# Order of choices, products and loads in the expert stage of a hybrid encoder layer

## The reference

```python
def _peer(hn, w_query, sub_keys, expert_u, expert_v):
    q = (hn @ w_query).reshape(B, S, PEER_HEADS, 2, PEER_HALF)
    s = jnp.einsum('bshpd,hpkd->bshpk', q, sub_keys)
    v1, i1 = lax.top_k(s[..., 0, :], PEER_TOPK)
    v2, i2 = lax.top_k(s[..., 1, :], PEER_TOPK)
    ...
    expert = e1 * N_KEYS + e2
    gate = jax.nn.softmax(cv, axis=-1)
    ...
        pre = jnp.einsum('tkd,td->tk', expert_u[it], xt)
        act = jax.nn.gelu(pre, approximate=False) * gt
        return jnp.einsum('tk,tkd->td', act, expert_v[it])
```

## Time and profile before

| | |
|---|---|
| three timed runs | 4036.6, 4049.0, 4050.2 µs; median 4049.0 |
| the profiled execution | 4044.4 µs, span 4042.7 µs |
| TensorE / its weight loads / VectorE / GpSimd / ScalarE busy | 92% / 79% / 66% / 48% / 31% |
| mean granted clock of TensorE | 0.964 |
| moved by DMA | 788.6 MB, mean 195 GB/s |

### The profile page before, as it was taken

The page is one execution under the profiler, slowest core; times in us unless marked ns, Lnnn a source line. Parts: engine busy times, 40 slices in busy tenths (PEclk is TensorE's granted clock), DMA queues, the critical chain, the costliest instruction groups (busy, mean ns, idle before and its releaser), DMA issues.

```text
span 4042.7 us, 55073 instructions
## 1 busy us (share of the span) xinstructions
PE 3721.7 (92%) x19212; PEld 3179.7 (79%) x19212; DVE 2684.3 (66%) x5197; ACT 1252.3 (31%) x1835; POOL 1939.3 (48%) x1352
## 2 busy tenths in 40 slices
PE   8978789999879899999999999999889999899998
PEld 6844478888767578799989999999667888677887
DVE  5443277776212437847878888788797666589996
ACT  3013233432211321233333333333233333333333
POOL 1023122222100013887878888888888888322220
PEclk9989889999989899999999999999889999999999
DMA  3259300000231024458888888888879999899996
GB/s 116 101 202 400 130 19 9 18 18 0 83 104 31 21 94 96 80 132 258 254 251 258 264 268 261 262 266 243 219 210 270 283 274 265 293 343 388 396 391 231
DMA packets 376333, 788.58 MB, mean 195 GB/s; under 512 B 137104, under 2 KB 245648, under 8 KB 342288
## 3 DMA queue, kind: packets, MB, share of 16 engines
q1 hardware_dynamic: 210320, 451.28, 32.8%
q0 software_dynamic: 165888, 336.01, 28.1%
HBM read 643.09 MB, written 144.05 MB: 195 GB/s over the span
## 4 chain that ended last, share of the span: by engine, by line
PE 28%; POOL 17%; issue 6%; DVE 5%; DMA 4%; DVEq 2%; ACT 1%; SPq 0%; POOLq 0%; ACTq 0%
PE peer_ps L2148 18%; POOL gates_d L2038 14%; PE peer_ps L2057 4%; PE peer_ps L2071 4%; POOL rows L2026 2%; POOL peer_rows L2026 2%; DMA peer_gat<-gates_d 2%; DMA rows<-in_expert_uv,peer_idx 1%; DMA late_in<-gates_d 1%; DVEq L2359 1%; PE peer_ps L2094 1%; DVE peer_acc L2444 1%; DVE late_rows L2429 1%; DVE late_in L2451 0%; DVEq L2443 0%
## 5 line engine op out<-in xcount | busy, mean ns | idle before, releaser
L2038 POOL DMA_INDIRECT gates_d<-peer_gates,peer_idx x768 | 1362.5, 1774 | 342.4 <-issue 222.8
L2057 PE MATMUL peer_ps<-high,peer_uh 128*128 128x384 f32 x2048 | 531.7, 340 | 58.3 <-DVE peer_ul L2346 51.7
L2057 PE MATMUL peer_ps<-low,peer_uh 128*128 128x384 f32 x2048 | 526.3, 338 | 0.0
L2057 PE MATMUL peer_ps<-high,peer_ul 128*128 128x384 f32 x2048 | 525.1, 337 | 0.0
L2057 PEld LDWEIGHTS peer_ps<-high,peer_uh 128*128 128x128 f32 x2048 | 371.3, 190 | 74.7 <-issue 67.5
L2057 PEld LDWEIGHTS peer_ps<-low,peer_uh 128*128 128x128 f32 x2048 | 375.3, 190 | 0.0
L2057 PEld LDWEIGHTS peer_ps<-high,peer_ul 128*128 128x128 f32 x2048 | 374.9, 190 | 0.0
L2148 PE MATMUL peer_ps<-peer_vh,peer_ah 128*128 128x512 f32 x1026 | 327.2, 401 | 46.0 <-DVE peer_al L2463 45.9
L2026 POOL DMA_INDIRECT late_rows<-in_expert_uv,peer_idx x108 | 135.9, 1258 | 407.4 <-DVE peer_acc L2444 365.0
L2148 PE MATMUL peer_ps<-peer_vh,peer_al 128*128 128x512 f32 x1026 | 323.2, 397 | 0.0
L2148 PE MATMUL peer_ps<-peer_vl,peer_ah 128*128 128x512 f32 x1026 | 321.7, 395 | 0.0
(11 more groups left out here) (470 smaller groups left out, 7694.9 us busy)
## 6 DMA issues: line engine op xcount, KB each, us to landing
late_in<-in_expert_uv SPq DMA_DIRECT2D x170, 512.0 KB, 4.9
gates_d<-mla_zeros POOLq DMA_DIRECT2D x128, 512.0 KB, 30.1
hidden_d<-peer_hid SPq DMA_DIRECT2D x128, 384.0 KB, 3.0
peer_raw<-in_expert_u SPq DMA_DIRECT2D x86, 512.0 KB, 4.9
peer_val<-in_expert_uv SPq DMA_DIRECT2D x86, 512.0 KB
late_in<-hidden_d SPq DMA_DIRECT2D x170, 192.0 KB, 5.3
late_in<-gates_d SPq DMA_DIRECT2D x170, 192.0 KB, 6.3
first_raw<-in_expert_u SPq DMA_DIRECT2D x42, 512.0 KB
```

Source lines behind the costliest of these rows:

```text
L2038: pool.indirect_dma_start(gates_flat, bass.IndirectOffsetOnAxis(ap=idx[:, n, k:k + 1], axis=0), gates[:, n, k:k + 1], None, compute_op=ALU ...
L2057: last = nc.tensor.matmul(ps[i][:, a, 0:HD], w[:, cols], x[:, kc, a * HD:(a + 1) * HD], start=(kc == 0 and w is uh[i % 2] and x is high), ...
```

## The change

- `unit_order`: within each head, the dense tiles come before the looked-up ones.
- `block_in` and `block_out`: all products of high by high parts (in `block_in` also low tokens by high weights) come first and wait for the high parts alone; the rest waits for the low parts.
- `load_out`: v and hidden values of block 129 (the second of pass 1) are loaded ahead of the gates of block 128.
- `halves(0)` and `others(0)`, the copies of pass 0's sums, stand one block sooner (before block 129's high parts instead of block 130's).
- Look-up 176, the first behind the last scatter, waits until block 129 is multiplied with its gates. The groups of rows from there on begin at slot 5 of pass 1 instead of 3 and come every 2.9 slots instead of 3.

```diff
@@ unit_order
-    return ([(head, tile) for head in range(PH) for tile in (looked_up if head < 5 else ()) + PASSES[0]]
-            + [(head, tile) for head in range(PH) for tile in (looked_up if head >= 5 else ()) + PASSES[1]])
+    return ([(head, tile) for head in range(PH) for tile in PASSES[0] + (looked_up if head < 5 else ())]
+            + [(head, tile) for head in range(PH) for tile in PASSES[1] + (looked_up if head >= 5 else ())])
@@ group_slot
-            return OUT + 13 + (g * 17) // 2 if g < PASS_SLOTS // GROUP else OUT + NK + 3 + 3 * (g - PASS_SLOTS // GROUP)
+            return OUT + 13 + (g * 17) // 2 if g < PASS_SLOTS // GROUP else OUT + NK + 5 + ((g - PASS_SLOTS // GROUP) * 29) // 10
@@ sync
-            def load_out(q):
+            def load_operands(q):
...
+            def load_gates(q):
...
                 if c == 0:
                     for tile in tiles:
                         sp.wait_ge(added[tile % 4], scatters(PH - 1, tile))
                 sp.dma_start(gat[r][:, 0:n], gates_d[c][:, tokens]).then_inc(in_ready[r], 16)
+            def load_out(q):
+                if q != NK + 1:
+                    load_operands(q)
+                if q == NK:
+                    load_operands(q + 1)
+                load_gates(q)
@@ gpsimd, look_up
+                if p == EARLY_SLOTS + PASS_SLOTS:
+                    pool.wait_ge(product, NK + 2)
@@ tensor
-            def block_in(i, first=False):
+            def block_in(i, block, first=False):
+                pe.wait_ge(u_high, block + 1)
                 for kc in range(KC):
...
-                    for w, x in ((uh[i % 2], high), (uh[i % 2], low), (ul[i % 2], high)):
+                    for x in (high, low):
                         for a in range(2):
...
+                pe.wait_ge(u_low, block + 1)
+                for kc in range(KC):
+                    for a in range(2):
+                        last = nc.tensor.matmul(ps[i][:, a, 0:HD], ul[i % 2][:, kc * P:kc * P + P],
+                                                high[:, kc, a * HD:(a + 1) * HD], start=False, stop=(kc == KC - 1))
...
+            def block_out(p, r, q, first_block=False, last_block=False):
...
+                pe.wait_ge(v_high, q + 1)
+                pe.wait_ge(a_high, q + 1)
+                for i in range(len(PASSES[p])):
+                    n = first + i
                     if first_block and n < 4:
                         pe.wait_ge(gelu_done, NK + n + 1)
                     if first_block and n >= 4:
                         pe.wait_ge(half_out, n - 3)
                         pe.wait_ge(other_out, n - 3)
...
+                    product(n, i, ah, vh)
+                pe.wait_ge(split_done, q + 1)
+                for i in range(len(PASSES[p])):
+                    n = first + i
+                    product(n, i, al, vh)
+                    last = product(n, i, ah, vl)
@@ scalar (and vector, with others(0))
-                if q == NK + RING - 1:
+                if q == NK + 1:
                     halves(0)
```

More of the change, by code:

```diff
@@ L2133, in _, with product @@
                 for i in range(4):
-                    pe.wait_ge(u_low, g * 4 + (WT + i + 1))
                     pe.wait_ge(gelu_done, g * 4 + (i + 1))
-                    block_in(i)
-            def block_out(p, r, first_block=False, last_block=False):
-                for i, tile in enumerate(PASSES[p]):
-                    n = p * len(PASSES[0]) + i
+                    block_in(i, g * 4 + (WT + i))
+            def block_out(p, r, q, first_block=False, last_block=False):
+                def product(n, i, x, w):
+                    for a in range(2):
+                        last = nc.tensor.matmul(ps[n % 4][:, a, :], x[r][:, i * P:(i + 1) * P],
+                                                w[r][:, a * HALF:(a + 1) * HALF],
+                                                start=(first_block and x is ah and w is vh),
+                                                stop=False, skip_group_check=True)
+                    return last
+                first = p * len(PASSES[0])
+                pe.wait_ge(v_high, q + 1)
+                pe.wait_ge(a_high, q + 1)
+                for i in range(len(PASSES[p])):
+                    n = first + i
                     if first_block and n < 4:
@@ L2532, in _ @@
             for q_out in range(1, 2 * NK):
-                if q_out == NK + RING - 1:
+                if q_out == NK + 1:
                     others(0)
```

37 lines of the change are left out of this document (13 added, 24 removed).

## The result

| | median, range (runs) | profiled execution, span |
|---|---|---|
| before | 4046.24 µs, 4036.02 to 4070.72 (14) | 4044.4, 4042.7 |
| after | 4016.83 µs, 4010.88 to 4036.64 (14) | 4013.74, 4012.2 |

The ratio is 0.9932, 95% interval [0.9916, 0.9949]: faster by 29.4 µs between the medians, 0.7%. I had predicted 54.9 µs. The direction held. The time lies outside the forecast's own range (3968 to 4008) and inside the wider one that reaches to 4025; the size did not hold.

What follows compares the result with a forecast made beforehand. GpSimd's chain of scatters and look-ups was taken to hold the expert_u stage's end and the pass border. 43.8 + 6.7 + 9.4 − 5 = 54.9 µs off 4044.4 gave 3990, range 3968 to 4008 (to 4025 with rivals).

Steps and rivals of the forecast that it cites:

- the wider one that reaches to 4025: Whole kernel: forecast range 3968 to 4008, extended to 4025 µs by including rivals of 0.10 each.
- 42.5 µs at the border: Gates load of block 128: issued at 3415.8 instead of 3458.3, as the new unit order shortens GpSimd's chain.
- 43.8 at the end: TensorE's start on block 128 at the pass border: 3422.5 instead of 3466.3, 43.8 µs earlier.
- just free: Look-up 8 in the expert_u stage: moved to 1832.0, its row 0 used at 1831.5, so no wait.
- 2812 predicted: End of the expert_u stage: 2860 less 42.5 for the order and 5.5 for starting on high parts.
- the 5.5 µs that I had for starting on the high parts: Expert_u stage: low weights needed only after 32 of a block's 48 matmuls, 5.5 µs later; slack counted once.
- VectorE's waits for rows: Expert_u stage: waits fall from 122 µs to some 80, with none before the middle of the stage.
- 6.7 µs** won: Border, first blocks of pass 1: third block starts 13.5 µs after the first instead of 20.2, 6.7 µs won.
- I count half, **9.4 µs: After the border, 3486.5 to 3653: half the time lost waiting for last low parts is hidden, 9.4 µs.
- load, split, next load: After the border: this loop does not contain TensorE, so a wait hidden by high parts may show up again.
- I take **5 µs: Pass 1 look-ups: price of 80 rows within 111 blocks, between 2 µs at 410 GB/s and 20 at 394.
- rival 4: Blocks 129 to 240: bytes move at only 346 GB/s as denser look-ups delay every load, 4062 µs; chance 0.04.

Runs made afterwards that it cites:

- order only: The kernel before with only the new unit order: 4007.52 µs against 4047.26, ratio 0.9895.
- first block as before: Changed kernel with look-ups of the kernel before, and the first block of block_in keeping high and low weights together: 4004.45 µs, ratio 0.9897.
- order and look-up edits: The kernel before with the new unit order, the hold of look-up 176 for block 129 and the new pace: 4011.51 µs, ratio 0.9925.
- rows one slot sooner: Changed kernel with the groups of early rows used from slot WT + 11 instead of WT + 12: 4023.02 µs, ratio 0.9935.
- order and border: The kernel before with the new unit order, block 129's operands ahead of block 128's gates and copies one block sooner: 4002.14 µs, ratio 0.9904.
- look-ups as before: Changed kernel without its two look-up edits (no hold, groups from slot 3 and 3 slots apart): 4003.37 µs, ratio 0.9885.
- all but the order: Changed kernel with the unit order of the kernel before: 4044.12 µs, ratio 0.9995.
- pace-only kernel: Changed kernel without the hold of look-up 176, keeping the new pace of 2.9 slots: 4004.31 µs, ratio 0.9898.
- small-row-work run: Changed kernel with VectorE's two operations on each looked-up row cut to 64 of 1024 columns: 3983.26 µs in one run.
- changed, hold for 131: Changed kernel with look-up 176 held for the product of block 131 instead of 129: 4003.15 µs, ratio 0.9899.
- hold for 133: Changed kernel with look-up 176 held for the product of block 133 instead of 129: 4009.55 µs against 4045.53, ratio 0.9906.
- look-ups two by two: Changed kernel with look-ups 176 to 181 released in twos, for the products of blocks 129, 130 and 131: 4018.75 µs, ratio 0.9928.
- hold for 128: Changed kernel with look-up 176 held for the product of block 128 instead of 129: 4011.78 µs, ratio 0.9930.

## Why the prediction was right in direction and too large

**The order of the units: the right steps, the size in part by luck.** I gave it 42.5 µs at the border and 43.8 at the end; alone it brought 39.7 by the medians, 42.5 by the ratio. But at the border the lead was 37.6, 28.8 and 31.0 µs in the three kernels that have the new order and the products as before (order only, with the look-up edits, with the border edits), and 26.1 to 31.9 in the seven that have the changed kernel's program up to there. In the traces of the first three the lead then grows by 5 to 16 µs in blocks 140 to 166, in a pattern that I had not booked to the order (below). The steps: first scatter 24.7 µs earlier (measured 24.6 and 24.7); both index waits gone (17.4 µs, measured so). What I called "just free" was not. Look-up 8 waits 2.79 µs with the order alone, and 6.84 once the products of high parts come first. The first `block_in` runs while VectorE still makes its low token parts, and the 16 matmuls with low weights now stand behind them instead of in between; row 0 is used 3.3 µs later (349.4 instead of 346.1 µs after the stage's first load; 346.0 again with the first block as before).

**The lead drifts, in the same program too.** With 24.6 + 17.4 − 6.85 the gates load should be 35.1 µs earlier in the changed kernel. At dense unit 12 it is on this line (35.7), at the last scatter 29.1. What is missing is a term for which I had put down nothing, a change in the issue times themselves. From the first scatter to the last the chain took 1879.1 µs before and 1874.6 in the changed kernel: 10.2 less idle and 2.2 less in the scatters, but 7.9 more in the 176 look-ups between them (214.0 before, 221.9 now, 217 to 229 in the other timed kernels). I first looked for the cause in the change. But the order-only kernel and the one with order and look-up edits have the same program up to the border, both stand at 39.1 µs at unit 12, and their gates loads come 37.6 and 28.8 µs earlier. Their scatters, the first line from the order-only kernel:

```profile
L2038 POOL DMA_INDIRECT gates_d<-peer_gates,peer_idx x768 | 1356.6, 1766 | 301.0 <-issue 220.7 <-DVE peer_idx L2416 67.8 <-DVE peer_acc L2444 12.2
```

```profile
L2040 POOL DMA_INDIRECT gates_d<-peer_gates,peer_idx x768 | 1365.7, 1778 | 301.0 <-issue 221.6 <-DVE peer_idx L2418 67.8 <-DVE peer_acc L2446 11.6
```

The idle time is the same and the look-ups between took 221.2 and 220.9 µs, so the 9 µs are 12 ns more in each of 768 scatters. The sum shows that the lengths make this drift; why they differ in the same program it doesn't show. The same sum tells where the wait of 6.85 µs at look-up 8 went with the rows one slot sooner: idle time 6.5 less, the look-ups' own issues 4.8 more, the scatters' 1.1 more, in all 0.6 µs gained. In the time, a few µs more or less at look-up 8 can't be seen in any case.

**The stage end: as late as the lead is short.** First output block at 2833.95, which is 2827.3 on before's clock, against 2812 predicted: 32.9 µs instead of 48. Look-up 147 came 30.7 µs earlier where I had 42.5, so 11.8 of the difference is the shorter lead; of the 5.5 µs that I had for starting on the high parts 2.2 came. VectorE's waits for rows came out at 76.6 µs where I had said 80 (122.2 before), but those over 1 µs start at 2145 already, not in the second half.

**The border: right at the border, gone ten blocks later.** I had the third block start 13.5 µs after the first instead of 20.2; it was 11.3. With these 8.9 µs TensorE is 42.1 µs ahead at the third block (the table's 43.0 is VectorE's multiply for it), where it was 33.2 at the first. I had booked such a lead as gain, with 9.4 µs more up to block 166. The step that failed is "**6.7 µs** won" and "I count half, **9.4 µs**": 16.1 µs predicted. Measured are −4 to 4 µs, which is nothing within these intervals: against the order only, with 39.7 µs by its medians and 42.5 by its ratio, order and border has 38.2 and 38.8, and look-ups as before, with the high parts first too, 43.9 and 46.5. The stretch says the same from inside: 65.3 µs with the order alone, 64.1 with the border edits, 64.0 with the high parts first too. I read it so that TensorE's early start does not help since the loop that decides there is the one I had named myself, load, split, next load, at 350 to 365 GB/s; no run took that loop apart. And blocks 140 to 166 took 107.2 µs with the order alone, where nothing around them was changed, 110.3 with all but the order, and 122.7 before: it seems that those waits come and go with the phase of loads and look-ups, and I had taken one pattern of them for a property of the program.

**The look-ups: the step with the wrong mechanism.** "I take **5 µs**" priced bytes over the whole of pass 1. The bytes were no problem: 393 GB/s over 280 µs with TensorE full, as before. The hold costs 10 to 14 µs (gain 29.4 with it and 39.1 in the pace-only kernel; ratios 0.9932 and 0.9898), both look-up edits together 11 to 19 (gains 28.8 against 39.7 and 29.4 against 43.9, and their ratios). Of these 8 to 10 stand in 12 blocks, because it moves 6 MB out of a time when the DMA had room (74 and 237 GB/s) into the time when three blocks' loads are urgent. Holding for block 131 instead takes 9 µs off the stretch and 8 (by gains) to 13 (by ratios) off the time. My rival 4, slower loads over the whole pass, was not it either.

By terms, what is missing: 1 to 4 µs of 43.8 for the order, 12 to 20 for the border and what follows, 5 to 14 for the look-ups, together 18 to 38; the forecast was 25.5 too high.

The Trainium skill (SBUF — State Buffer, section "SBUF: two separate sides") says that a VectorE operation with two SBUF inputs and a GpSimd operation that reads SBUF hold the port pair that they share one after the other, and that the later one is blocked until the other has ended. The small-row-work run agrees in direction (1785 ns to 1601 ns with two-input operations cut short). That GpSimd can't write the descriptors of its transfers meanwhile, the section says of another kind of VectorE operation (its 2-port perf modes); whether it is what lengthens the scatters here no run shows. Measured is the lengthening alone, 0.18 µs in the mean.

**The best version.** Ratios and stretches go together; the medians come from different sessions (before: the median of the kernel before in the same one):

| kernel | stretch | median | before | ratio |
|---|---|---|---|---|
| look-ups as before | 64.0 | 4003.4 | 4047.3 | 0.9885 |
| order only | 65.3 | 4007.5 | 4047.3 | 0.9895 |
| first block as before | 64.3 | 4004.5 | 4043.4 | 0.9897 |
| pace only | 64.0 | 4004.3 | 4043.4 | 0.9898 |
| changed, hold for 131 | 64.9 | 4003.2 | 4040.3 | 0.9899 |
| order and border | 64.1 | 4002.1 | 4040.3 | 0.9904 |
| hold for 133 | 69.7 | 4009.6 | 4045.5 | 0.9906 |
| order and look-up edits | 73.0 | 4011.5 | 4040.3 | 0.9925 |
| look-ups two by two | 73.3 | 4018.8 | 4043.4 | 0.9928 |
| hold for 128 | 71.6 | 4011.8 | 4040.3 | 0.9930 |
| changed | 73.9 | 4016.8 | 4046.2 | 0.9932 |
| rows one slot sooner | 73.8 | 4023.0 | 4047.3 | 0.9935 |

The first seven cannot be told apart by their ratios. Two lines, the new order, give what can be had from this change; the hold should go, or wait for block 131. The row with 69.7 shows that the stretch is not all.

**What stays open.** Which transfer stands behind which inside the DMA engines I read from times to landing, not from a record of the queues. Why the scatters take 12 ns more in one execution of the same program than in another, 9 µs in all, is not settled. And blocks 140 to 166 took 107 to 123 µs in these profiles, in a pattern that no edit here was aimed at.

## What to carry to other kernels

A start that comes earlier is only won if the chain behind it is the one that was late: when TensorE starts early into a stretch that loads decide, the time comes back some blocks later. So book a gain at the end of the disturbed stretch, not at its first block. Before deferring a batch of transfers, look at what the DMA moves in the place they leave and in the place they go to; their place relative to the next urgent loads matters more than their bytes (4 µs later was worth 8 to 13 µs). And before explaining a difference of a few µs between two profiles, compare two kernels that share the program up to that point.

## What I had not expected of the hardware

- GpSimd's scatters (issue of an indirect DMA) took 1785 ns in the mean from 1880 to 2800 µs, and 1601 with VectorE's row operations cut to a sixteenth, with nothing changed on GpSimd.
- The loads of one queue alone moved 237 GB/s in 5 µs at the start of pass 1 (DMA share 0.75, changed kernel; 285 and 0.83 in the same window of the one with the hold for block 131), together with the look-ups of the other 416 (share 1.03, pace only).
- The same program up to the border reached it 37.6, 31.0 and 28.8 µs ahead in three executions, and the changed kernel's 26.1 to 31.9 µs ahead in seven.
